# Second block: activations and products moved a few words along their buffers, by another amount in each stage

## Chip, cores and metric

One NeuronCore of one Trainium2 chip runs the whole program. The metric is device time in microseconds (us) of one execution; each kernel is timed several times and the median is given.

## The reference, cut to what matters

Two networks of two layers run one after the other on the same hidden state of 272 tokens (16 meta tokens and 256 others) by 1024 features. The second one, on the last 256 tokens, is the part that the change touches. For each of its layers:

```
h = h + 0.5 * swiglu(rmsnorm(h, g1), w_gate, w_up, w_down)      # ffn1, 1024 -> 2816 -> 1024
p = rmsnorm(h, g2) @ w_in                                       # 1024 -> 2048
h = h + mixer(p) @ w_out                                        # pooling, Fourier and attention heads
h = h + 0.5 * swiglu(rmsnorm(h, g3), w_gate2, w_up2, w_down2)   # ffn2
```

The first network (the "first block" below) has the same shape of work with 272 tokens, layer norms and another mixer.

## The kernel before

Activations lie transposed: 128 features in the partitions, tokens along the free axis, in 8 chunks for the 1024 features (`KD`) and 22 for the 2816 of the hidden layer (`NF`). A weight block of 128 by 128 is the stationary operand, an activation chunk of 128 by 256 tokens the moving one.

Every large product is made in float32r from parts. A value is split into `hi` (the value rounded to float32r) and `lo` (what is left of it), and each product of a chunk is three matmuls into the same accumulator (`three`, L620 to L624): w_lo with x_hi (L622), w_hi with x_lo (L623), w_hi with x_hi (L624). ScalarE makes the `hi` parts, VectorE the `lo` parts, of the weights as they come from HBM (double buffered in `raw`, `w_hi`, `w_lo`) and of the activations once for each stage.

A feed-forward layer has an "up" stage (22 pairs of blocks, gate and up, 8 chunks each: 22 x 2 x 8 x 3 = 1056 matmuls) that reads `x_hi` and `x_lo`, and a "down" stage (8 blocks of 22 chunks: 528 matmuls) that reads `hid_hi` and `hid_lo`, the products silu(gate) * up. The input projection has 16 blocks of 8 chunks (384 matmuls) and reads `x_hi`, `x_lo`; small float32 matmuls of the mixer are put in between its blocks by hand. The output projection (192 matmuls) reads another place of the hidden buffers. The stages of the second block in their order are up4, down4, in0, out0, up5, down5, up6, down6, in1, out1, up7, down7, where the number is `q`, the count of feed-forward layers since the start. The first two pairs of up4 are done on operands that are levelled afterwards (`plain`, 96 matmuls); the other 960 read `x_hi` and `x_lo`.

Each engine runs one list of instructions in program order with semaphores between them. TensorE waits for `x_ready` chunk by chunk at the start of a stage, for `lo_done` (the weights of a unit), `up_free` (a PSUM bank emptied) and `hid_ready`.

Where things lie is fixed by the order of allocation. `LINE` (L208) is 16 words, 64 bytes, and the buffers are spaced by gaps of one or two of them. In the second block a chunk is 256 words long and the next follows at once:

```
xt_hi, xt_lo = chunks(x_hi_all, KD, T2), chunks(x_lo_all, KD, T2)
hidt_hi, hidt_lo = chunks(hid_hi_all[:, HID_HI_T2:], NF, T2), chunks(hid_lo_all[:, HID_LO_T2:], NF, T2)
```

In each partition, in units of 64 bytes, `w_hi` begins at 610, `w_lo` at 964, the second block's `x_hi` at 1317, `x_lo` at 1465, its `hid_hi` at 2817 and its `hid_lo` at 3193. A weight block is 8 units long, a chunk of 256 tokens 16 units. So each float32r operand of the kernel, weights and activations, begins at a multiple of 64 bytes, and in the second block activations begin at an odd unit and weights at an even one. In the first block a chunk is 272 tokens (17 units) or, with columns beside it, 274, at a pitch of 17 or 18 units, and its starts are multiples of 64 bytes too. In one of its stages the three matmuls of a chunk have 258, 256 and 260 columns (L629 to L632). The constants `cst` begin 32 bytes past such a multiple; float32 matmuls read them, among them the transposes of L1182, whose moving operand is the identity at the start of `cst`.

`x_of` (L301) and `hid_of` (L307) give the pair of views that all three engines use for a stage.

Of the kernel before, what the change touches and what calls it, by code (L numbers as in the profile page):

```python
# [195 lines left out]
def build(nc, hidden0, w_up, w_down, w_in1, w_out1, w_in2, w_out2, prm1, prm2, consts, out):  # L196
    with ExitStack() as ctx:
# [103 lines left out]
        def x_of(T):  # L301
            return {T1: (x1_hi, x1_lo), T2: (xt_hi, xt_lo)}.get(T, (x_hi, x_lo))
# [4 lines left out]
        def hid_of(T):  # L307
            return (hidt_hi, hidt_lo) if T == T2 else (hid_hi, hid_lo)
# [307 lines left out]
        def _(pe):  # L616
# [83 lines left out]
            def up(q, turn0, event, T, before={}, opening=False):  # L700

                pe.wait_ge(up_free, q * NF + (CREDIT - 1))
                if opening:
                    opening_pair()
                else:
                    first_pair(turn0, event, 0, T)
                pe.wait_ge(up_free, q * NF + CREDIT)
                for u in range(2):
                    narrow_unit(turn0, 1, u, ps[:, 2 + u, 0:T], T, before=before if u == 0 else {})
                with pe.Fori(0, (UP_T - 1) // 2) as half:  # L710
                    for i in range(4):
# [3 lines left out]
                        for u in range(2):  # L715
                            narrow_unit(turn0 + half * 2 + (1 + i // 2), j, u, ps[:, 2 * j + u, 0:T], T,
# [28 lines left out]
            def crossing_up(q, turn0, event, norm, T):  # L745
# [9 lines left out]
                first_pair(turn0 + 1, event, 0, T, None, {k + 2: lambda k=k: first_square(k) for k in range(KD - 2)})  # L755
                last_squares()
                pe.wait_ge(up_free, q * NF + (CREDIT + 2))
                for u in range(2):
                    narrow_unit(turn0 + 1, 1, u, ps[:, 2 + u, 0:T], T)
                with pe.Fori(2, UP_T) as it:  # L760
                    for j in range(2):
                        pe.wait_ge(up_free, q * NF + it * 2 + (j - 1 + CREDIT))
                        for u in range(2):
                            narrow_unit(turn0 + it, j, u, ps[:, 2 * j + u, 0:T], T)
# [48 lines left out]
            def down(q, turn0, resid, T):  # L813
                ha, hb = hid_of(T)
# [278 lines left out]
            def mixer2(l, turn0, event, norm):  # L1093

                def block(i):
# [3 lines left out]
                    narrow_unit(turn0 + i // 4, (i // 2) % 2, i % 2, ps[:, i % IN_BANKS, 0:T2], T2)  # L1099
# [109 lines left out]
                first_pair(turn0, event, 0, T2)  # L1209
# [82 lines left out]
        def _(act):  # L1292
# [39 lines left out]
            def first_cast(it, j, T):  # L1332
# [3 lines left out]
                fn(hid_of(T)[0][:, f, 0:T], src, ACT.Copy).then_inc(first_casts, 1)  # L1336
# [26 lines left out]
            def high(table, gain, k, T, N):  # L1363

                fn(x_of(N)[0][:, k, 0:T], h[:, k, T1 - T:T1], ACT.Identity, scale=par(table, gain, k)).then_inc(xh_ready, 1)
# [30 lines left out]
            def down(turn0, resid, rms, norm, T, gain=None):  # L1396
                def turn(it, next_width):
                    for j in range(2):
                        split_next(turn0 + it, j, W_WIDE if j == 0 else next_width)
                        end = next_width == W_NARROW and j == 1  # L1400
                        if end and rms:

                            for k in range(KD - 1):
                                high(P2, gain, k, T, T2)
# [5 lines left out]
                        if end and rms:  # L1410
                            high(P2, gain, KD - 1, T, T2)
# [5 lines left out]
            def out_proj(turn0, resid, rms, norm, T, gain=None):  # L1417
                for p in range(OUTB // 2):
# [3 lines left out]
                    if rms and last:  # L1422

                        for k in range(KD):
                            if k >= 2 * p:
                                act.wait_ge(resid_ready, resid * KD + (k + 1 + CREDIT))
                            high(P2, gain, k, T, T2)
# [71 lines left out]
            def level_up(q, turn0, level, T):  # L1499
# [6 lines left out]
                def pair(it, j, width):  # L1506
# [11 lines left out]
                    fn(hid_of(T)[0][:, f, 0:T], prod[:, j:j + 1, 0:T], ACT.Copy).then_inc(cast_done, 1)  # L1518
# [37 lines left out]
            def crossing_up(q, turn0, T):  # L1556
# [11 lines left out]
                high(P1, "firstg", 0, T, T)  # L1568
                split_hi(turn0 + 1, 0, W_NARROW)
                for k in (1, 3, 5):  # L1570
# [3 lines left out]
                    for c in (k, k + 1):  # L1574
                        high(P1, "firstg", c, T, T)
# [1503 lines left out]
```

## Time and profile before

| | |
|---|---|
| time, median of 3 runs | 1949.19 us (1948.94 to 1949.41) |
| span of the profiled execution, first to last instruction | 1945.9 us |
| what the median has beyond that span | 3.3 us |
| TensorE busy | 1931.2 us, 99% |
| VectorE busy | 1431.5 us, 74% |
| ScalarE busy | 1019.8 us, 52% |
| mean granted TensorE clock | 0.999 |

The page gives the span of the profiled execution and no device time of its own for it. A stage is read best from the number of matmuls that start in a stretch of time: a matmul's own duration in the rows (0.28 us) overlaps its neighbours', and the distance from start to start is what it costs. The second block's stages lie about here in the span: up4 1059 to 1168 us, down4 to 1227, in0 to 1287, out0 to 1310, up5 1322 to 1442, down5 to 1501, up6 to 1621, down6 to 1681, in1 to 1735, out1 to 1757, up7 1769 to 1889, down7 to the end.

### The profile page before, as it was taken

What the parts mean: (1) busy time and instruction counts of PE and PEld (TensorE: products, weight loads), DVE (VectorE), ACT (ScalarE), POOL (GpSimd) and SP (SyncE); (2) the same over time, 40 slices, a digit from 0 to 9 for tenths busy, and PEclk for the clock granted to TensorE, in tenths of its full rate; (3) what the DMA queues carried; (4) which work ended last, traced back from release to release, by engine and by line L of the source; (5) the groups of instructions that cost most, each with busy time, mean ns of one, the idle gap of its engine ahead of it and who ended that gap; (6) DMA issues with size and microseconds to landing.
All of it is one profiled execution on the core that took longest, in us unless ns stands there. A gap on an engine that the chain in (4) does not pass through costs nothing.

```text
span 1945.9 us, 42335 instructions
## 1 busy us (share of the span) xinstructions
PE 1931.2 (99%) x16150; PEld 1892.7 (97%) x16150; DVE 1431.5 (74%) x2591; ACT 1019.8 (52%) x1527; POOL 152.7 (8%) x192
## 2 busy tenths in 40 slices
PE   9999999999999999999999999999999999999998
PEld 8999989999999999899999999999999999999998
DVE  6774787987588768879978874667765775667763
ACT  4443687554455447865547443665445444565443
POOL 0001123000100011320010100000000000100000
PEclk9999999999999999999999999999999999999999
DMA  7454433545454544345553665445555555435554
GB/s 265 172 197 170 166 109 112 192 174 193 156 192 172 196 164 145 109 152 194 201 191 140 235 233 183 151 149 185 193 214 177 195 202 208 152 131 195 194 213 154
DMA packets 46830, 346.66 MB, mean 178 GB/s; under 512 B 5344, under 2 KB 6416, under 8 KB 9232
## 3 DMA queue, kind: packets, MB, share of 16 engines
q1 hardware_dynamic: 44416, 335.63, 48.0%
q0 software_dynamic: 2320, 9.74, 1.6%
q8 instruction: 63, 1.03, 0.2%
q14 instruction: 31, 0.25, 0.0%
HBM read 344.29 MB, written 1.07 MB: 177 GB/s over the span
## 4 chain that ended last, share of the span: by engine, by line
PE 91%; DVE 4%; ACT 2%; DVEq 1%; issue 1%; DMA 0%; ACTq 0%; SPq 0%; POOL 0%
PE ps L622 22%; PE ps L623 22%; PE ps L624 22%; PE ps L639 14%; PE ps L630 2%; PE ps L631 2%; PE ps L632 2%; DVE w_lo L1996 1%; PE ps L1162 0%; DVE pj L2465 0%; DMA h<-in_hidden 0%; DVE cst L2486 0%; PE ps L1197 0%; DVE pj L2462 0%; ACT scratch L1669 0%
## 5 line engine op out<-in xcount | busy, mean ns | idle before, releaser
L1996 DVE TENSOR_TENSOR w_lo<-raw,w_hi 128x1024 fp32r<-128x1024 f32 (+1 forms) x582 | 749.3, 1313 | 151.1 <-ACT w_hi L1300 91.5
L622 PE MATMUL ps<-x_hi,w_lo 128*128 128x256 f32 (+3 forms) x2208 | 622.1, 282 | 1.5 <-DVE x_lo L2087 0.6
L624 PE MATMUL ps<-x_hi,w_hi 128*128 128x256 f32 (+3 forms) x2208 | 615.1, 279 | 0.0
L623 PE MATMUL ps<-x_lo,w_hi 128*128 128x256 f32 (+3 forms) x2208 | 614.8, 278 | 0.0
L1297 ACT ACTIVATE w_hi<-raw 128x1024 fp32r<-128x1024 f32 x454 | 466.3, 1052 | 92.5 <-PE ps L639 49.0
L622 PE MATMUL ps<-hid_hi,w_lo 128*128 128x256 f32 (+1 forms) x1536 | 431.5, 281 | 0.1
L624 PE MATMUL ps<-hid_hi,w_hi 128*128 128x256 f32 (+1 forms) x1536 | 430.2, 280 | 0.0
L623 PE MATMUL ps<-hid_lo,w_hi 128*128 128x256 f32 (+1 forms) x1536 | 429.8, 280 | 0.0
L622 PEld LDWEIGHTS ps<-x_hi,w_lo 128*128 128x128 f32 x2208 | 414.9, 188 | 6.4 <-issue 4.2
L623 PEld LDWEIGHTS ps<-x_lo,w_hi 128*128 128x128 f32 x2208 | 415.0, 188 | 0.5
L624 PEld LDWEIGHTS ps<-x_hi,w_hi 128*128 128x128 f32 x2208 | 414.6, 188 | 0.0
L622 PEld LDWEIGHTS ps<-hid_hi,w_lo 128*128 128x128 f32 x1536 | 288.7, 188 | 2.6 <-DVE hid_lo L2731 1.4
L624 PEld LDWEIGHTS ps<-hid_hi,w_hi 128*128 128x128 f32 x1536 | 288.8, 188 | 0.0
L623 PEld LDWEIGHTS ps<-hid_lo,w_hi 128*128 128x128 f32 x1536 | 288.3, 188 | 0.0
L639 PE MATMUL ps<-plain,w_hi 128*128 128x274 f32 x1280 | 211.6, 287 | 0.0
L1348 ACT ACTIVATE silu<-silu 128x256 f32<-128x256 f32 (+1 forms) x108 | 45.3, 420 | 270.6 <-DVE silu L2010 270.5
L639 PEld LDWEIGHTS ps<-plain,w_hi 128*128 128x128 f32 x1280 | 179.9, 188 | 0.0
L1300 ACT ACTIVATE w_hi<-raw 128x1408 fp32r<-128x1408 f32 x128 | 169.0, 1368 | 3.6 <-PE ps L624 2.5
L639 PE MATMUL ps<-plain,w_lo 128*128 128x274 f32 x640 | 131.7, 287 | 0.0
L639 PEld LDWEIGHTS ps<-plain,w_lo 128*128 128x128 f32 x640 | 100.1, 188 | 0.0
L2099 DVE SCALAR_TENSOR_TENSOR h<-h,ps 128x256 f32<-128x256 f32 (+2 forms) x72 | 30.0, 422 | 94.3 <-PE ps L624 94.2
L630 PE MATMUL ps<-plain,w_lo 128*128 128x258 f32 x352 | 98.2, 284 | 0.0
(351 smaller groups left out, 2315.3 us busy)
## 6 DMA issues: line engine op xcount, KB each, us to landing
raw<-in_w_up SPq DMA_DIRECT2D x176, 1024.0 KB, 4.8
raw<-in_w_down SPq DMA_DIRECT2D x64, 1408.0 KB, 6.0
raw<-in_w_in SPq DMA_DIRECT2D x36, 1024.0 KB, 4.8
raw<-in_w_out SPq DMA_DIRECT2D x16, 1024.0 KB, 4.8
cst<-row_copy POOLq DMA_DIRECT2D x2, 1088.0 KB, 8.5
raw<-in_w_up SPq DMA_DIRECT2D x4, 512.0 KB, 7.2
cst<-in_consts POOLq DMA_DIRECT2D x1, 1537.5 KB, 6.5
prm<-in_prm POOLq DMA_DIRECT2D x2, 690.0 KB, 7.2
```

The lines of the kernel that those rows point to most:

```text
L622: mm(dst, low, xa, start=first, stop=False)
L623: mm(dst, high, xb, start=False, stop=False)
L624: return mm(dst, high, xa, start=False, stop=last)
L630: mm(dst[:, 0:T2 + 2], low, xa[:, 0:T2 + 2], start=False, stop=False)
L631: step = mm(dst[:, 0:T2], high, xb[:, 0:T2], start=False, stop=False)
L632: return step if first else mm(dst, high, xa, start=False, stop=last)
L639: last = mm(dst, w[:, c, :], x[:, c, 0:T], start=w is low and c == 0, stop=w is high and x is xa and c == KD - 1)
L1297: fn(narrow_at(w_hi, place, j, u), narrow_raw(j, u), ACT.Copy).then_inc(hi_done, 1)
L1300: fn(w_hi[:, j, c], raw[:, j, c], ACT.Copy).then_inc(hi_done, 1)
L1348: fn(silu[:, j, 0:T], silu[:, j, 0:T], ACT.Silu).then_inc(silu_done, 1)
L1996: v.tensor_tensor(dst, src, high.bitcast(F32), ALU.subtract).then_inc(lo_done, 1)
L2099: v.scalar_tensor_tensor(out=dst, in0=dst, scalar=alpha, in1=ps[:, bank:bank + 1, 0:T], op0=ALU.mult, op1=ALU.add).then_inc(resid_ready, 1)
```

## The change

`x_of` and `hid_of` get the name of the stage and, for the stages in two tables, begin their views some words further on in the same buffers. Producers (ScalarE's `high` and casts, VectorE's `low` and the hid parts) and TensorE use the same views. No instruction is added or taken away, no wait is changed, and lengths and pitches stay.

| stage | hi part moved by | lo part moved by |
|---|---|---|
| up4, without its first two pairs | 32 bytes | 32 bytes |
| in0 | 16 | 16 |
| up5 | 48 | 48 |
| up6 | 96 | 96 |
| in1 | 8 | 8 |
| up7 | 32 | 0 |
| down5 | 32 | 32 |
| down6 | 16 | 16 |
| down7 | 0 | 32 |

Weights, down4, both output projections and the first block stay where they are.

```diff
+        X_WORDS = {"up4": (8, 8), "in0": (4, 4), "up5": (12, 12), "up6": (24, 24), "in1": (2, 2), "up7": (8, 0)}
+        HID_WORDS = {5: (8, 8), 6: (4, 4), 7: (0, 8)}
+
-        def x_of(T):
+        def x_of(T, stage=None):
+            if T == T2 and stage:
+                high, low = X_WORDS[stage]
+                return chunks(x_hi_all[:, high:], KD, T2), chunks(x_lo_all[:, low:], KD, T2)
             return {T1: (x1_hi, x1_lo), T2: (xt_hi, xt_lo)}.get(T, (x_hi, x_lo))
...
-        def hid_of(T):
+        def hid_of(T, q):
+            if T == T2 and q in HID_WORDS:
+                high, low = HID_WORDS[q]
+                return chunks(hid_hi_all[:, HID_HI_T2 + high:], NF, T2), chunks(hid_lo_all[:, HID_LO_T2 + low:], NF, T2)
             return (hidt_hi, hidt_lo) if T == T2 else (hid_hi, hid_lo)
...
+                xs = x_of(T, None if opening else f"up{q}")
...
-                    first_pair(turn0, event, 0, T)
+                    first_pair(turn0, event, 0, T, xs)
...
-                    narrow_unit(turn0 + i // 4, (i // 2) % 2, i % 2, ps[:, i % IN_BANKS, 0:T2], T2)
+                    narrow_unit(turn0 + i // 4, (i // 2) % 2, i % 2, ps[:, i % IN_BANKS, 0:T2], T2, x_of(T2, f"in{l}"))
...
-                fn(x_of(N)[0][:, k, 0:T], h[:, k, T1 - T:T1], ACT.Identity, scale=par(table, gain, k)).then_inc(xh_ready, 1)
+                fn(x_of(N, stage)[0][:, k, 0:T], h[:, k, T1 - T:T1], ACT.Identity, scale=par(table, gain, k)).then_inc(xh_ready, 1)
...
-                down(t0 + SEC2["ffn1"] + UP_T, r0, True, s0, T2, "mixg")
+                down(t0 + SEC2["ffn1"] + UP_T, r0, True, s0, T2, "mixg", f"in{l}")
```

The rest of the diff hands the stage's name down to `high` and `low` and to TensorE's `crossing_up`, `down` and `mixer2`.

## Rows read from the trace of the kernel before

**Rows 1.** The page: busy time of each engine; granted TensorE clock in forty slices.

```profile
PE 1931.2 (99%) x16150; PEld 1892.7 (97%) x16150; DVE 1431.5 (74%) x2591; ACT 1019.8 (52%) x1527; POOL 152.7 (8%) x192
...
PEclk9999999999999999999999999999999999999999
```

**Rows 2.** The page: shares of the chain that ended last, by engine.

```profile
PE 91%; DVE 4%; ACT 2%; DVEq 1%; issue 1%; DMA 0%; ACTq 0%; SPq 0%; POOL 0%
```

**Rows 3.** Windows of ten stretches of the second block: bounds, length, busy time (instructions) per engine, clock, DMA, GB/s.

```profile
1070.00:1160.00 90.00, 90.00 (x796) 90.00 (x796) 71.17 (x123) 41.07 (x52) 7.04 (x13) 1.00 0.67 231
1170.00:1225.00 55.00, 55.00 (x488) 55.00 (x487) 28.48 (x30) 25.33 (x30) 4.46 (x6) 1.00 0.52 188
1230.00:1285.00 55.00, 55.00 (x451) 52.17 (x450) 40.35 (x97) 32.91 (x71) 3.33 (x2) 1.00 0.41 151
1325.00:1440.00 115.00, 115.00 (x1017) 115.00 (x1016) 88.95 (x145) 51.73 (x64) 0.00 (x0) 1.00 0.58 207
1445.00:1500.00 55.00, 55.00 (x485) 54.95 (x485) 28.59 (x32) 27.04 (x35) 5.77 (x8) 1.00 0.52 184
1505.00:1620.00 115.00, 115.00 (x1017) 115.00 (x1016) 88.56 (x144) 51.17 (x63) 0.00 (x0) 1.00 0.57 203
1625.00:1680.00 55.00, 55.00 (x485) 54.95 (x484) 29.08 (x35) 27.16 (x36) 6.00 (x8) 1.00 0.50 182
1685.00:1735.00 50.00, 50.00 (x399) 46.23 (x399) 35.04 (x88) 29.46 (x68) 0.00 (x0) 1.00 0.43 154
1770.00:1885.00 115.00, 115.00 (x1017) 115.00 (x1016) 90.19 (x148) 51.96 (x63) 0.00 (x0) 1.00 0.58 204
1890.00:1938.00 48.00, 47.96 (x422) 47.55 (x420) 19.62 (x18) 19.53 (x24) 4.45 (x6) 1.00 0.45 164
```

**Rows 4.** Timeline of TensorE, first and last of 37 matmuls in a row.

```profile
1099.76 0.28 PE L622 MATMUL ps<-x_hi,w_lo 128*128 128x256 f32 x1
...
1103.84 0.28 PE L622 MATMUL ps<-x_hi,w_lo 128*128 128x256 f32 x1
```

**Rows 5.** Windows of five stretches of the first block.

```profile
40.00:120.00 80.00, 80.00 (x649) 80.00 (x648) 58.22 (x96) 32.86 (x41) 0.00 (x0) 1.00 0.51 182
160.00:200.00 40.00, 40.00 (x323) 40.00 (x322) 17.08 (x16) 13.63 (x15) 7.55 (x10) 1.00 0.45 161
360.00:440.00 80.00, 80.00 (x651) 80.00 (x650) 70.03 (x140) 42.71 (x56) 0.00 (x0) 1.00 0.51 184
560.00:620.00 60.00, 60.00 (x479) 60.00 (x478) 51.77 (x102) 31.22 (x41) 0.00 (x0) 1.00 0.51 179
880.00:940.00 60.00, 60.00 (x507) 60.00 (x506) 54.82 (x110) 32.14 (x44) 0.00 (x0) 1.00 0.53 191
```

**Rows 6.** Timeline of TensorE in the input projection, around two groups of float32 matmuls.

```profile
1269.25 0.60 PE L1182 MATMUL ps<-cst,scratch 128*128 128x128 f32 x4
1269.69 1.03 PE L1197 MATMUL ps<-scratch 128*128 128x256 f32 x4
1270.55 0.38 PE L1172 MATMUL ps<-cst,pj 128*128 128x128 f32 x2
...
1270.89 0.28 PE L623 MATMUL ps<-x_lo,w_hi 128*128 128x256 f32 x1
...
1271.61 0.28 PE L623 MATMUL ps<-x_lo,w_hi 128*128 128x256 f32 x1
...
1272.19 0.28 PE L622 MATMUL ps<-x_hi,w_lo 128*128 128x256 f32 x1
...
1273.43 0.28 PE L624 MATMUL ps<-x_hi,w_hi 128*128 128x256 f32 x1
```

**Rows 7.** VectorE groups by line, 1080 to 1160 us: busy, mean ns, idle before.

```profile
L2012 DVE SCALAR_TENSOR_TENSOR prod<-ps,rstd 128x256 f32<-128x256 f32 x15 | 6.4, 424 | 10.1 <-PE ps L624 10.1
...
L2041 DVE TENSOR_TENSOR hid_lo<-prod,hid_hi 128x256 f32 x14 | 6.0, 426 | 2.4 <-issue 2.4
L2039 DVE CAST hid_hi<-prod 128x256 f32 (+1 forms) x15 | 4.4, 294 | 2.8 <-issue 2.7
```

More of the change, by code:

```diff
@@ L1403, in turn @@
                             for k in range(KD - 1):
-                                high(P2, gain, k, T, T2)
+                                high(P2, gain, k, T, T2, stage)
                         if end:
@@ L1410, in turn @@
                         if end and rms:
-                            high(P2, gain, KD - 1, T, T2)
+                            high(P2, gain, KD - 1, T, T2, stage)
                 with act.Fori(0, DOWN_T - 1) as it:
@@ L2082, in up, with low @@
                 turn(UP_T - 1, W_WIDE)
-            def low(number, table, gain, k, T, N):
-                xa, xb = x_of(N)
+            def low(number, table, gain, k, T, N, stage=None):
+                xa, xb = x_of(N, stage)
                 dve.wait_ge(xh_ready, number * KD + (k + 1))
@@ L2219, in level_up, with down @@
                 pair(UP_T - 1, 1, None)
-            def down(turn0, alpha, T, number=None, gain=None):
+            def down(turn0, alpha, T, number=None, gain=None, stage=None):
                 def turn(it, next_width):
@@ L2228, in turn @@
                             for k in range(KD - 1):
-                                low(number, P2, gain, k, T, T2)
+                                low(number, P2, gain, k, T, T2, stage)
                         if end:
@@ L2238, in down @@
                 if gain:
-                    low(number, P2, gain, KD - 1, T, T2)
+                    low(number, P2, gain, KD - 1, T, T2, stage)
             def last_down(turn0):
@@ L2251, in last_down, with out_proj @@
                 turn(DOWN_T - 1, True)
-            def out_proj(turn0, alpha, T, banks, number=None, gain=None):
+            def out_proj(turn0, alpha, T, banks, number=None, gain=None, stage=None):
                 for p in range(OUTB // 2):
@@ L2260, in out_proj @@
                             for k in ((0, 1, 2), (3,))[u]:
-                                low(number, P2, gain, k, T, T2)
+                                low(number, P2, gain, k, T, T2, stage)
                         elif last and u == 1:
@@ L2267, in out_proj @@
                     for k in range(4, KD):
-                        low(number, P2, gain, k, T, T2)
+                        low(number, P2, gain, k, T, T2, stage)
                     lo_unit(turn0 + OUTB // 4, 1, 0, W_NARROW)
```

49 lines of the change are left out of this document (25 added, 24 removed).

## The prediction

> **What bounds the kernel.** I read the page's first two parts before anything else. TensorE is busy 99% of the span and its granted clock stands at 9 tenths or more in every slice [rows 1], so the clock is not in play, and the chain that ended last is TensorE for 91% [rows 2]. A change that touches neither the number of matmuls nor a wait can then move the time in one way: by what one matmul costs from start to start. So the views that matter are the windows, which count matmuls in a stretch, and the timeline.
>
> In the second block the count is the same wherever only float32r products run: 1017 matmuls in each of three stretches of 115 us in up5, up6 and up7, 796 in 90 us in up4, 485 in 55 us in down5 and down6 [rows 3]. The exact distance is read from the timeline: 36 matmuls from 1099.76 to 1103.84 us, 4.08 / 36 = 113.3 ns [rows 4]. At 2.4 GHz, the level that the full granted clock means, 256 columns take 106.7 ns, so 6.6 ns of each matmul are no column time. In the input projections the count is lower (451 in 55 us, 399 in 50 us) since longer float32 matmuls stand between.
>
> **What the change can touch.** Counting the matmuls whose moving operand is moved: up4 960, up5, up6 and up7 3 x 1056 = 3168, in0 and in1 2 x 384 = 768, down5, down6 and down7 3 x 528 = 1584; together 6480. One nanosecond on each is 6.5 us of the whole, and 0.2% of the time, 3.9 us, which is about what a measurement of this kernel can tell from no change, is 0.6 ns on each. So the whole prediction is: what happens to these 6.6 ns when a moving operand begins 8, 16, 32, 48 or 96 bytes further on.
>
> **The parts that cost nothing.** The same number of instructions is issued, the transfers don't change, and no wait is added, so nothing is queued anew on SP's or POOL's queue. ScalarE and VectorE write and read the moved views with instructions of unchanged shape. No row shows a store at such an offset, so I bound it: VectorE's two operations on the hidden parts take 0.43 and 0.29 us for each of the pairs, and ahead of the same pair's up product it waits 10.1 us in 15 pairs for TensorE, 0.67 us each [rows 7]. They would have to double before TensorE noticed. If that cover were gone, each tenth of their time would be 0.07 us for each of 3 x 22 pairs, 5 us. I take 0, and nothing speaks for a gain here, as VectorE is not what sets the end.
>
> **The part that may cost: the moving operand's phase.** No row of before has a float32r operand off a multiple of 64 bytes. The nearest rows give these bounds.
>
> First, that distances between the operands matter at all. The first block's stages run with the same three matmuls and other distances of 64-byte units: 649 matmuls of 272 columns in 80 us are 123.3 ns each, 10.0 above their 113.3 of columns; 323 in 40 us are 123.8, 10.5 above; 651 of 274 columns in 80 us 122.9, 8.7 above their 114.2; 479 in 60 us 125.3, 11.1 above; and 507 of 258, 256 and 260 in 60 us 118.3, 10.8 above the mean of 107.5 [rows 5]. Against 6.6 in the second block that is 2.1 to 4.5 ns more. Two streams read at once, the moving operand and the weights of the next matmul, and how they meet has a price.
>
> Second, that the price is not a property of one address alone. After float32 matmuls in in0 the float32r ones run at (1271.61 - 1270.89) / 6 = 120 ns for a while, and then at (1273.43 - 1272.19) / 11 = 113 ns, in the same block, at the same kind of addresses [rows 6]. The pair of streams starts out of step and slides into a place where it collides less. In a stage of chunks of 256 columns each matmul repeats the phase of the one before, so a place once found is kept for thousands of matmuls. A shift by a part of 64 bytes changes where the moving stream steps from one 64-byte unit to the next; if the streams can slide, they find a place again at the same price. The second block gives that price in `x` stages and in `hid` stages, which have different distances to the weights (1317 and 2817 against 964, in units). That is the reason for my value: 0 ns.
>
 Put on 6480 matmuls it is 10.4 us. It has a second use: 1.7 ns is the least that a matmul costs above its columns here, so at most 6.6 - 1.7 = 4.9 ns are to be won, 4.9 x 6480 = 32 us.
>
> Fourth, the far end: a chunk of 1024 bytes that begins inside a unit touches 17 units instead of 16. If a unit costs its 16 columns' time however little of it is used, that is 6.7 ns, 43 us in all.
>
> On the resettling after float32 groups in in0 and in1: one case costs about 6 x 6.7 = 40 ns, the kernel puts some 18 groups into each projection, 0.7 us; halved or doubled it is 1 us at most over both, inside the noise.
>
> The Trainium skill, "TensorE: Matmul & The Clock Gate", section "Back-to-back issue gap", gives a warm gap of N / 2.4 + 2.5 ns, 109.2 for 256 columns. This trace has 113.3, so here it does not hold as it stands; an estimate by it of what shifts could win at best is 4.1 x 6480 = 27 us.
>
> The same skill, "SBUF — State Buffer", section "Door 1: The DMA port swizzle", says that SBUF lines are 16 bytes long and that each step to a new line costs. By it a shift of a multiple of 16 bytes changes nothing, as a chunk still covers 64 lines, and only in1, at 8 bytes, touches a 65th. No run here shows it yet. It sides with my value, and it would set in1 apart, which has 384 of the 6480 matmuls.
>
> **The sum.** Span 1945.9 us, with 0 for the stores and 0 for the 6480 matmuls: 1945.9. The median has 3.3 us beyond the span, so 1949.2.
>
> **The rivals.**
>
> *A start inside a unit has a small price of its own.* For: four rows of L1182 read 1.6 ns more than L1197. Against: the reading is coarse and the stream there is half as fast. Time: 0.6 to 2 ns, 4 to 13 us, so 1953 to 1962. Chance 0.17.
>
> *The streams collide as in the first block.* The shifted moving operand and the weights meet in the pattern of the first block's stages and stay in it, since each matmul repeats the phase. For: five stages of the first block, each dearer. Against: there chunk lengths or pitches are other than 16 units, so phases wander; in the second block they do not. Time: 2.1 to 4.5 ns on all, 14 to 29 us, so 1963 to 1978. It decides the sign from 0.6 ns on, or from about a fifth of the matmuls at 3 ns. Chance 0.15.
>
> *A seventeenth unit is paid in full.* Time: 6.7 ns on each would be 43 us, 1992; in up7 a third of the matmuls and in down7 two thirds read an unmoved part, 704 in all, which takes off 5 us: 1988. Against: in the first block 274 columns, which touch 18 units, cost no more above their columns than 272, which touch 17 (8.7 and 11.1 against 10.0 and 10.5). Chance 0.08.
>
> *Faster: the 6.6 ns are themselves a collision that a shift inside the unit opens.* Every distance so far is a whole number of units, and half a unit might let weights and activations pass between each other. For: 1.7 ns suffices for a slow stream, and even the best float32r stretch has 6.6. Against: 6.6 is met in stages with different distances, like a floor of this stream. If all stages gained all, 1917; the amounts differ by stage, so a half of it, or half of the stages, is the likelier, 1933, and a quarter 1941. Chance 0.22.
>
> **How the numbers follow.** No change has 0.38 and is the likeliest single case, with its own range of 1945.3 to 1953.1. The slower rivals together have 0.17 + 0.15 + 0.08 = 0.40, the faster one 0.22. The range leaves out 0.08 below 1937, the greater part of a full gain, and 0.1 above 1984, the full seventeenth unit and a bit of collisions worse than the first block's: 1937 to 1984. Different stages may go different ways, and then the sum lies inside.
>
> **What the profile of the changed kernel would show.** Windows over the same ten stretches, set to the stages' new places, are the test: 1017 matmuls in 115 us means no change in that stage; 978 would be 4.3 ns more, 1056 as much less. Down4 must stay at 488 in 55 us, being unmoved. If the price hangs on the shift, up5 (48), up6 (96) and up7 (32 and 0) will differ, though they are the same work; if it hangs on crossing a 16-byte line, only in1 moves. Up7 and down7 tell by lines L622 to L624 whether it is the moved part alone that pays. Wrong would be the idea that the streams slide into an equally good place: a steady distance other than 113.3 ns in a moved stage, with TensorE still without waits. A longer wait for `x_lo` or `hid_lo` before a stage would show that the stores were dearer, which I exclude.

## The result, and the profile after

The changed kernel takes 1981.79 us (median of 4, 1979.47 to 1981.96) against 1949.3 for the kernel before (median of 4): 1.0166 times as long, 95% interval 1.0151 to 1.018. I had forecast no change. The time lies inside my range, on the side of the slower rivals.

The page has nothing to explain it but TensorE itself, 35 us more busy time at the same clock (against [rows 1]):

```profile
PE 1966.4 (99%) x16150; PEld 1927.9 (97%) x16150; DVE 1431.8 (72%) x2591; ACT 1019.6 (51%) x1527; POOL 152.8 (8%) x192
...
PEclk9999999999999999999999999999999999999999
```

The windows over the same ten stretches, set to the stages' new places, answer to [rows 3]; columns as there:

```profile
1075.00:1160.00 85.00, 85.00 (x720) 85.00 (x720) 63.72 (x107) 37.45 (x48) 6.94 (x13) 1.00 0.62 216
1180.00:1235.00 55.00, 55.00 (x486) 55.00 (x485) 29.97 (x31) 25.68 (x32) 5.19 (x7) 1.00 0.47 167
1237.00:1292.00 55.00, 55.00 (x439) 52.16 (x438) 39.95 (x97) 31.67 (x68) 3.32 (x2) 1.00 0.40 147
1330.00:1445.00 115.00, 115.00 (x974) 115.00 (x973) 87.27 (x147) 50.76 (x63) 0.00 (x0) 1.00 0.53 191
1455.00:1510.00 55.00, 55.00 (x467) 55.00 (x466) 29.12 (x31) 24.74 (x31) 5.19 (x7) 1.00 0.44 163
1520.00:1635.00 115.00, 115.00 (x969) 115.00 (x969) 86.60 (x144) 51.28 (x62) 0.00 (x0) 1.00 0.54 193
1645.00:1700.00 55.00, 55.00 (x465) 55.00 (x464) 27.83 (x30) 24.13 (x30) 5.18 (x7) 1.00 0.45 162
1705.00:1760.00 55.00, 55.00 (x428) 51.79 (x427) 38.90 (x94) 30.34 (x68) 2.30 (x2) 1.00 0.39 136
1795.00:1910.00 115.00, 115.00 (x988) 115.00 (x987) 88.79 (x149) 52.35 (x65) 0.00 (x0) 1.00 0.55 197
1922.00:1970.00 48.00, 48.00 (x403) 48.00 (x402) 18.33 (x16) 19.52 (x24) 4.45 (x6) 1.00 0.45 164
```

Down4 in the second line, which was not moved, has 486 matmuls in 55 us where before had 488, with a count that is good to one or two. Every moved stage has fewer: up4 720 in 85 us, where before has 796 in 90, up5 974 in 115 us for 1017, up6 969, up7 988, down5 and down6 467 and 465 in 55 us for 485, down7 403 in 48 us for 422. VectorE's (DVE) and ScalarE's (ACT) share of the span falls with it, and nobody waits for anything new.

Two things said of before have to be set right for this reading. A window counts the matmuls that are running in it, not only those that start in it, so two or three that were under way at its beginning are in the count: 1017 in 115 us is (115 + 0.28) / 1017 = 113.4 ns, and 974 is 118.4. And up5, down5, up6, down6 and up7 begin some 11 us earlier in the span of before than was said (up5 at 1311 us, down5 1431, up6 1491, down6 1611, up7 1757, down7 1877), so that the stretches of [rows 3] for up5 to down6 and up7 hold some 9 us of the stage behind them. In before the price there is the same within 1 ns, so the counts stand. The stretches shown below for other kernels also reach up to 13 us into the next stage; the prices in the text don't, they are taken from the records of one stage alone.

From the start times of all records of a stage (distances over 160 ns, which are a wait or another matmul in between, are left out) the mean distance from one matmul to the next is, in ns:

| stage | moved by (hi, lo), bytes | before | after | stage longer by, us |
|---|---|---|---|---|
| up4 | 32, 32 | 113.6 | 118.3 | 4.5 |
| down4 | 0, 0 | 113.3 | 113.4 | 0.0 |
| in0 | 16, 16 | 114.1 | 118.8 | 1.7 |
| up5 | 48, 48 | 113.4 | 118.3 | 5.2 |
| down5 | 32, 32 | 113.3 | 118.3 | 2.7 |
| up6 | 96, 96 | 113.4 | 118.9 | 5.9 |
| down6 | 16, 16 | 113.3 | 118.9 | 2.9 |
| in1 | 8, 8 | 114.1 | 121.3 | 2.7 |
| up7 | 32, 0 | 113.4 | 116.7 | 3.5 |
| down7 | 0, 32 | 113.3 | 120.0 | 3.5 |

The sum is 32.6 us, 5.0 ns on each of the 6480 matmuls. The spans differ by 34.2 (1980.1 and 1945.9); the other 1.6 us are in the first block, which the change does not touch, and they are a difference of two parts. The profiled execution of before waited 1.1 us longer in its first microseconds; the first line is before's, the second the changed kernel's:

```profile
PE ps L677 <- DVE x_lo L2812: 1.5, 1, 1.5
PE ps L686 <- DVE x_lo L2823: 0.4, 1, 0.4
```

Against it stand about 2.6 us more in one up stage of the first block. There the profiled executions fell on two sides of something that the program does with and without the change. The changed kernel has:

```profile
380.00:440.00 60.00, 60.00 (x478) 60.00 (x478) 50.36 (x99) 30.57 (x40) 0.00 (x0) 1.00 0.49 177
560.00:620.00 60.00, 60.00 (x479) 60.00 (x477) 51.70 (x105) 31.52 (x41) 0.00 (x0) 1.00 0.49 175
```

The first of these stretches has 489 matmuls in the kernel before. I come back to it at the end.

In down7 only the lo part was moved. The lines L622 to L624 of before are L631 to L633 in the changed kernel. From L632, w_hi with hid_lo, the next matmul starts 0.13 us later, from its neighbours 0.12:

```profile
1932.16 0.28 PE L633 MATMUL ps<-hid_hi,w_hi 128*128 128x256 f32 x1
1932.28 0.28 PE L631 MATMUL ps<-hid_hi,w_lo 128*128 128x256 f32 x1
1932.40 0.28 PE L632 MATMUL ps<-hid_lo,w_hi 128*128 128x256 f32 x1
1932.53 0.28 PE L633 MATMUL ps<-hid_hi,w_hi 128*128 128x256 f32 x1
```

Over the stage it is 124 ns after L632, 119 after L631 and 117 after L633. So the matmul that reads the moved part pays most, but the two that read an unmoved one pay too, 4 to 6 ns above before's 113.3. How the price is shared among the three lines is not fixed: with the same addresses down7 of the eighth experiment below has 121, 118 and 114. The stage's mean is what to read.

### The profile page after: what moved, and what is told of

Read it like the earlier page. It is cut to its first block, busy times and chain, and to the rows that moved or that the text cites. A ratio compares the mean times of both kernels' runs of the same rounds, so it can differ in the third digit from the quotient of the medians.

```text
span 1980.1 us, 42335 instructions
## 1 busy us (share of the span) xinstructions
PE 1966.4 (99%) x16150; PEld 1927.9 (97%) x16150; DVE 1431.8 (72%) x2591; ACT 1019.6 (51%) x1527; POOL 152.8 (8%) x192
## 4 chain that ended last, share of the span: by engine, by line
PE 91%; DVE 4%; ACT 2%; DVEq 1%; issue 1%; ACTq 0%; DMA 0%; SPq 0%; POOL 0%
PE ps L631 22%; PE ps L633 22%; PE ps L632 22%; PE ps L648 14%; PE ps L639 2%; PE ps L640 2%; PE ps L641 2%; DVE w_lo L2007 1%; PE ps L1173 0%; DVE pj L2476 0%; DVE cst L2497 0%; PE ps L1208 0%; DVE pj L2473 0%; ACT scratch L1680 0%; DVE scratch L2442 0%
## 5 line engine op out<-in xcount | busy, mean ns | idle before, releaser
L631 PE MATMUL ps<-x_hi,w_lo 128*128 128x256 f32 (+3 forms) x2208 | 630.3, 285 | 1.5 <-DVE x_lo L2098 0.6
L633 PE MATMUL ps<-x_hi,w_hi 128*128 128x256 f32 (+3 forms) x2208 | 623.3, 282 | 0.0
L632 PE MATMUL ps<-x_lo,w_hi 128*128 128x256 f32 (+3 forms) x2208 | 622.1, 282 | 0.0
L1308 ACT ACTIVATE w_hi<-raw 128x1024 fp32r<-128x1024 f32 x454 | 466.2, 1052 | 111.7 <-PE ps L648 50.3
L631 PE MATMUL ps<-hid_hi,w_lo 128*128 128x256 f32 (+1 forms) x1536 | 434.6, 283 | 0.1
L632 PE MATMUL ps<-hid_lo,w_hi 128*128 128x256 f32 (+1 forms) x1536 | 433.3, 282 | 0.0
L633 PE MATMUL ps<-hid_hi,w_hi 128*128 128x256 f32 (+1 forms) x1536 | 432.4, 282 | 0.0
L631 PEld LDWEIGHTS ps<-x_hi,w_lo 128*128 128x128 f32 x2208 | 415.6, 188 | 6.3 <-issue 4.2
L632 PEld LDWEIGHTS ps<-x_lo,w_hi 128*128 128x128 f32 x2208 | 417.2, 189 | 0.5
L633 PEld LDWEIGHTS ps<-x_hi,w_hi 128*128 128x128 f32 x2208 | 415.6, 188 | 0.0
L631 PEld LDWEIGHTS ps<-hid_hi,w_lo 128*128 128x128 f32 x1536 | 288.9, 188 | 2.5 <-DVE hid_lo L2742 1.3
L633 PEld LDWEIGHTS ps<-hid_hi,w_hi 128*128 128x128 f32 x1536 | 290.1, 189 | 0.0
L632 PEld LDWEIGHTS ps<-hid_lo,w_hi 128*128 128x128 f32 x1536 | 288.6, 188 | 0.0
L2023 DVE SCALAR_TENSOR_TENSOR prod<-ps,rstd 128x256 f32<-128x256 f32 (+1 forms) x108 | 46.1, 427 | 82.7 <-PE ps L633 82.7
L1385 ACT ACTIVATE pj<-h (+1 forms) x48 | 19.7, 417 | 157.7 <-DVE h L2110 157.7
```

The costliest lines, as they stand in the source:

```text
L631: mm(dst, low, xa, start=first, stop=False)
L632: mm(dst, high, xb, start=False, stop=False)
L633: return mm(dst, high, xa, start=False, stop=last)
L1308: fn(narrow_at(w_hi, place, j, u), narrow_raw(j, u), ACT.Copy).then_inc(hi_done, 1)
L2023: v.scalar_tensor_tensor(out=half, in0=upb[:, 0:T], scalar=0.5, in1=rstd[:, 0:T], op0=ALU.mult, op1=ALU.mult).then_inc(up_free, 1)
```

## The experiments

Four theories were open after the result. A: a start inside a 64-byte unit costs, whatever the weights do. A16: crossing a 16-byte line costs. B: the distance between the moving operand and the weights costs. S: any move off the old placement costs. Since the stages up5, up6 and up7 are the same work, and down4 to down7 too, one kernel can try another placement in each. Each kernel but the last is the changed one with the edit shown. Prices below are mean distances in ns as in the table. Experiments 1 to 6 and 9 to 11 were executed once each. How good such a price is can be seen from the stages that were left alone: up and down stages of 256 columns at the old distance have 113.3 to 113.6 in every run that has them, input projections 114.0 to 114.4.

### 1. Whole units of 64 bytes

```diff
-        X_WORDS = {"up4": (8, 8), "in0": (4, 4), "up5": (12, 12), "up6": (24, 24), "in1": (2, 2), "up7": (8, 0)}
-        HID_WORDS = {5: (8, 8), 6: (4, 4), 7: (0, 8)}
+        X_WORDS = {"up4": (0, 0), "in0": (0, 0), "up5": (16, 16), "up6": (32, 32), "in1": (0, 0), "up7": (16, 0)}
+        HID_WORDS = {4: (16, 16), 5: (32, 32), 6: (16, 0), 7: (0, 16)}
```

> Activations are moved by whole units of 64 bytes alone: up5 by one unit (hi and lo), up6 by two, up7 the hi part by one, down4 by one, down5 by two, down6 the hi part by one, down7 the lo part by one; up4, in0, in1 not at all. Theory A (a start inside a 64-byte unit is what costs): every stage stays at 113.3 ns for each matmul, and the time is 1949 us. Theory B (the distance between the moving operand and the weights is what costs, and 64 bytes matter as parts of them do): up6 and down5, moved by an even number of units, stay at 113.3; up5, up7 and down4, down6, down7, where activations and weights now begin at units of the same parity, go to 117 to 125 ns, and the time to some 1965 us.

Measured 1974.11 us. Up4 and the input projections were back at 113.5 and 114.1 to 114.2. Up5 and down4 (64 bytes) took 119.1, up6 and down5 (128 bytes) 118.9, up7 and down6 (hi part by 64) 117.8, down7 (lo part by 64) 117.8. Theory A is out: aligned starts cost as much as misaligned ones. B stands, but not as I had put it, for by it 128 bytes should have been free.

### 2. Small amounts

```diff
+        X_WORDS = {"up4": (1, 1), "in0": (8, 8), "up5": (4, 4), "up6": (8, 8), "in1": (8, 8), "up7": (14, 14)}
+        HID_WORDS = {4: (1, 1), 5: (2, 2), 6: (12, 12), 7: (14, 14)}
```

> Both parts moved by 4 bytes (up4, down4), 8 (down5), 16 (up5), 32 (up6, in0, in1), 48 (down6) and 56 (up7, down7). Theory A (any start inside a 64-byte unit costs the same, since a chunk then touches 17 units): all moved stages at 118 to 119 ns. Theory A16 (crossing 16-byte lines costs beside it): 16, 32 and 48 bytes at 118 to 119, and 4, 8 and 56 bytes dearer by 2 to 3 ns, 121, as in1 was in the changed kernel. Theory B (the phase between the two streams): the price rises and falls with the amount, so 4 bytes would be near 113.3 to 114 and 32 bytes the most. By each the two input projections, moved by 32 bytes here, come to about 118 ns between their float32 groups. Time 1978 to 1990 us.

Measured 1989.86 us. Multiples of 16 bytes: 118.9 (16), 118.3 (32 in up6, 118.4 and 118.3 in in0 and in1), 118.3 (48). Others: 121.2 and 121.5 (4 bytes), 121.6 (8), 120.2 and 120.0 (56). So the price jumps with the first 4 bytes and does not grow with the amount, and what is not a multiple of 16 bytes costs some 1 to 3 ns more. A16 had foreseen this, beside the larger price. Whether it comes from lines of 16 bytes or from the distance to the weights is not shown, as no run moved activations and weights together by such an amount. In1 of the changed kernel, moved by 8 bytes, had 121.3 and comes down to 118.3 here at 32.

### 3. The weights moved instead

```diff
+        sb("gapw", [P, LINE // 2])
         w_hi = sb("w_hi", [P, 2, 2 * W_WIDE], F32R)
...
-        sb("gap0", [P, LINE])
+        sb("gap0", [P, LINE // 2])
...
+        X_WORDS = {"up4": (0, 0), "in0": (8, 8), "up5": (8, 8), "up6": (0, 0), "in1": (0, 0), "up7": (4, 4)}
+        HID_WORDS = {4: (0, 0), 5: (8, 8), 6: (12, 12), 7: (16, 16)}
```

> Both weight buffers are moved 32 bytes further on in the whole program; activations: up5, in0 and down5 moved 32 bytes too, so that their distance to the weights is the old one; up4, up6, in1 and down4 not moved; up7 by 16 bytes, down6 by 48, down7 by 64. Theory A (the moving operand's own start costs): up4, up6, in1 and down4, down7 at 113.3 ns, up5, down5, up7, down6 at 118 to 119, whatever the weights do; the first block as before. Theory B (the distance to the weights costs): up5, down5 at 113.3 and up4, up6, down4 at 118 or more, and the first block changes too. A third possibility, each stream pays for its own misplaced start: up6 and up4 about 118, up5 and down5 more than either, 120 to 124.

Measured 1978.16 us. Windows of up5, down5 and up6 (115, 50 and 115 us):

```profile
1335.00:1450.00 115.00, 115.00 (x1017) 115.00 (x1016) 91.11 (x151) 52.64 (x65) 0.00 (x0) 1.00 0.56 203
1455.00:1505.00 50.00, 50.00 (x443) 50.00 (x442) 27.27 (x29) 22.87 (x28) 4.47 (x6) 1.00 0.49 177
1515.00:1630.00 115.00, 115.00 (x979) 115.00 (x978) 87.39 (x147) 50.69 (x63) 0.00 (x0) 1.00 0.53 191
```

Up5 and down5, whose activations and weights are both off by 32 bytes, have the old 1017 matmuls in 115 us: 113.4 and 113.3 ns. Up6, whose activations lie where they always did, has 979: 117.8, as have up4 and down4. Down6 is a distance of +16 bytes and takes 118.9, down7 +32 and takes 118.3, the same as those distances cost in the second experiment. Up7 is -16 bytes and takes 117.8. This is theory B without a remainder: the distance to the weights counts, and the moving operand's own address does not.

### 4. Fewer columns

```diff
                 xs = x_of(T, None if opening else f"up{q}")
+                T = {5: 248, 6: 248, 7: 240}.get(q, T)
...
                 ha, hb = hid_of(T, q)
+                T = {5: 248, 6: 248, 7: 240}.get(q, T)
...
+        X_WORDS = {"up4": (0, 0), "in0": (0, 0), "up5": (0, 0), "up6": (8, 8), "in1": (0, 0), "up7": (0, 0)}
+        HID_WORDS = {5: (0, 0), 6: (8, 8), 7: (8, 8)}
```

> Leaves out the last 8 or 16 tokens of the matmuls of four feed-forward layers' stages (their results are left as they were in PSUM): up5 and down5 248 columns from an unmoved start, up6 and down6 248 columns from a start moved by 32 bytes (which end on a 64-byte boundary and touch 16 units), up7 240 columns from an unmoved start, down7 240 from a start moved by 32 bytes (it touches 16 units). Above the time of the columns (103.3 ns for 248, 100.0 for 240) before has 6.6 ns. Theory A1 (a chunk pays for each unit touched, 17 in place of 16): up6 and down6 have 16 units and cost no more than up5 and down5. Theory A2 (a start inside a unit costs by itself): up6 and down6 keep 11 to 12 ns above their columns, 115, and up5 is 110. Theory A3 (an end inside a unit costs as a start does): up5 and down5 are 11 to 12 above too. Up7 is 106.7 by each if nothing but full units matters; an odd number of units could cost more by theory B.

This kernel leaves out a part of the work; its time was 1950.58 us. 248 unmoved columns took 113.3 ns, exactly what 256 take; 248 moved by 32 bytes 115.6; 240 unmoved 111.9, 240 moved 112.2. None of the three theories had foreseen that 8 columns less save nothing. So the 6.6 ns that I had counted as the moving stream's own are not a surcharge on its columns.

### 5. The period

```diff
+        X_WORDS = {"up4": (192, 192), "in0": (64, 64), "up5": (64, 64), "up6": (128, 128), "in1": (80, 80), "up7": (48, 48)}
+        HID_WORDS = {4: (64, 64), 5: (48, 48), 6: (128, 128), 7: (80, 80)}
```

> Both parts moved by 256 bytes (up5, in0, down4), 512 (up6, down6), 768 (up4), 192 (up7, down5) and 320 (in1, down7). In the runs so far the price hung on the distance between activations and weights alone, and 64 and 128 bytes cost as much as 32. Before holds 113.3 ns for all chunks, though from one chunk to the next the distance changes by 512 bytes, and `x` and `hid` stages differ by 256 in the distance of their hi parts. Theory P256 (the phase repeats after 256 bytes): 256, 512 and 768 at 113.3, 192 at 117 to 119, 320 as the 64 bytes of the second experiment's up5, 119.1. Theory P512: 512 at 113.3, and 256 and 768 at 117 to 121. Theory S (any move off the placement before costs, whatever its size): all at 118 to 119. Time: 1961 us by P256, 1972 by P512, 1980 by S.

Measured 1962.14 us. Windows of up5, up6 and up7, 110 us each:

```profile
1325.00:1435.00 110.00, 110.00 (x972) 110.00 (x971) 87.52 (x147) 51.72 (x63) 0.00 (x0) 1.00 0.56 202
1505.00:1615.00 110.00, 110.00 (x973) 110.00 (x972) 86.88 (x145) 49.85 (x63) 0.00 (x0) 1.00 0.56 200
1775.00:1885.00 110.00, 110.00 (x932) 110.00 (x931) 82.89 (x142) 48.26 (x61) 0.00 (x0) 1.00 0.53 190
```

256 bytes (up5, down4), 512 (up6, down6) and 768 (up4) are free: 113.3 to 113.6. 192 bytes costs 118.4, 320 costs 119.1, as 64 did. The price repeats after 256 bytes. Theory S is out. It is also clear now why all chunks of a stage could have one price: from chunk to chunk the distance grows by 512 bytes, two periods.

### 6. Far fewer columns

```diff
+                T = {5: 192, 6: 128, 7: 224}.get(q, T)
...
+        X_WORDS = {"up4": (0, 0), "in0": (0, 0), "up5": (0, 0), "up6": (0, 0), "in1": (0, 0), "up7": (0, 0)}
+        HID_WORDS = {5: (8, 8), 6: (8, 8), 7: (8, 8)}
```

The line with `T` stands in the same two places as in the fourth experiment.

> Leaves out the last tokens in the matmuls of six stages (their results stay as they were in PSUM): 192 columns in up5 and down5, 128 in up6 and down6, 224 in up7 and down7; up stages not moved, down stages moved by 32 bytes. In the run with 248 columns the unmoved stage stayed at 113.3 ns, as with 256, which the moving stream alone can't explain. Theory W (loading the next weights sets the pace, and the moving stream only disturbs it): 128, 192 and 224 columns all lie between 107 and 113 ns, well above their column times of 53, 80 and 93, and the moved stages stand 0 to 5 ns above the unmoved, less with fewer columns, as there is less to collide with. Theory M (each matmul costs its columns and a fixed 6 to 7 ns, and 248 was a coincidence of phase): 60, 87 and 100 ns.

This kernel too leaves out a part of the work; its time was 1938.48 us. Windows of up5 (192 columns) and up6 (128), 110 us each:

```profile
1320.00:1430.00 110.00, 110.00 (x987) 110.00 (x986) 88.70 (x150) 51.91 (x65) 0.00 (x0) 1.00 0.57 205
1500.00:1610.00 110.00, 110.00 (x988) 110.00 (x986) 88.42 (x145) 51.18 (x62) 0.00 (x0) 1.00 0.57 208
```

987 and 988 matmuls in 110 us: 111.6 ns with 192 columns and with 128, where the columns alone are 80 and 53 ns. Up7, with 224, took 111.7, and so did down5 to down7, moved by 32 bytes. The loads of weights (PEld) keep this pace themselves; these two rows of up5 are the first and the last of ten, nine distances in 1.01 us:

```profile
1319.97 0.19 PEld L631 LDWEIGHTS ps<-x_hi,w_lo 128*128 128x128 f32 x1
...
1320.98 0.19 PEld L631 LDWEIGHTS ps<-x_hi,w_lo 128*128 128x128 f32 x1
```

Is it the loads that set the pace, or a least distance between any two matmuls? The trace of before has a pair of float32 matmuls with 2 moving columns each:

```profile
1238.70 0.30 PEld L1107 LDWEIGHTS ps<-pj,cst 128*128 128x128 f32 x2
1238.81 0.28 PE L1107 MATMUL ps<-pj,cst 128*128 128x2 f32 x2
```

By their start times the two loads are 112 ns apart and the two matmuls 31. So matmuls can start closer together, and loads of this size have the distance of 112 here too. Not every load has this distance: in the float32 transposes of L877 the loads, 128 columns of 64 rows, start 58 to 65 ns apart. For float32r with 128 to 224 columns I therefore take the load as what sets the pace of 111.7 ns, and there a bad distance costs nothing. What the second block pays is this pace; the moving stream adds 1.7 ns to it at the good distance and 6 to 7 at a bad one (both parts moved, by a multiple of 16 bytes), once it fills the time between two loads. The Trainium skill, "TensorE: Matmul & The Clock Gate", section "LDWEIGHTS (loading the stationary operand)", has a load take its columns divided by 1.2, 106.7 ns for 128; the pace measured here is 5 ns above that.

### 7 and 8. The halves of the change

The seventh keeps `X_WORDS` of the change and empties `HID_WORDS`, the eighth the other way round.

> Only the `x` part of the change (up4, in0, up5, up6, in1, up7), `hid` as before. If each stage pays for its own move, as the stages of the changed kernel read: 4.5 + 1.7 + 5.2 + 5.9 + 2.7 + 3.5 = 23.5 us, so 1973 us, ratio 1.012. If a part of it is made by the neighbours (a later start that collides with something else), the two halves don't add up to the whole.

> Only the `hid` part of the change (down5, down6, down7). By the stages of the changed kernel 2.7 + 2.9 + 3.5 = 9.1 us, so 1958 us, ratio 1.005.

Against before at a median of 1946.86 (8 runs): the `x` half 1970.43, ratio 1.0117 (1.01 to 1.0134), the `hid` half 1954.99, ratio 1.004 (1.0026 to 1.0054). That is 23.6 and 8.1 us, where 23.5 and 9.1 were expected; together 31.7. In the eighth down7 took 117.8 ns, where the whole change had 120.0 with the same addresses, 1.2 us over the stage; down5 took 118.9 for 118.3. A bad distance thus has more than one steady pattern.

### 9 and 10. Another distance between the weight buffers

```diff
-        sb("gap", [P, 2 * LINE])
+        sb("gap", [P, 3 * LINE])
...
+        X_WORDS = {"up4": (48, 48), "in0": (0, 0), "up5": (0, 0), "up6": (16, 16), "in1": (16, 16), "up7": (32, 32)}
+        HID_WORDS = {4: (0, 0), 5: (16, 16), 6: (32, 32), 7: (48, 48)}
```

This is the ninth; the tenth has `4 * LINE`.

> The gap between the weight buffers is one unit of 64 bytes longer, so w_lo and all that lies behind it (the activations too) are one unit further from w_hi. The activations of the second block then run through all four unit phases: moved by 0 (up5, down4), 1 (up6, down5), 2 (up7, down6) and 3 units (up4, down7). By the runs so far the phase of 256 bytes decides. Theory P (what meets is the moving stream of one matmul and the weight load of the next, so both w_hi and w_lo have a best phase against the activations): with w_hi and w_lo no longer two units apart, a phase that suits w_hi misses w_lo or the other way round, and no stage gets back to 113.3; the best is 115 to 117, the worst 121. Theory W (only the distance to one of the two weight buffers matters): one of the four phases gives 113.3. The first block changes in part: its stages at 123 to 126 ns move by 1 to 4 ns either way.

> The same with two units more between the weight buffers, so that w_hi and w_lo lie at the same phase of 256 bytes; activations again at all four phases. Theory P: one phase of four suits both buffers, and as good as before, 113.3 ns; the others 118 to 121. Theory D (the two weight buffers must be two units apart, as before has them, because consecutive weight loads would meet each other): no phase gives 113.3. If any gives less, towards the 111.7 ns that weight loads alone took in the run with fewer columns, there is a version faster than both kernels: 1.6 ns on 8000 matmuls, 13 us.

Let a phase be the place in a period of four units of 64 bytes, and let (a, b) mean that the activations are a units past w_hi and b past w_lo in it. Before is (3, 1). Ninth, 1982.77 us: (0, 1) 117.8; (1, 2) 115.6; (2, 3) 117.8 in down6 and 118.7 in up7; (3, 0) 117.8. Tenth, 1982.58 us: (1, 1) 117.8; (2, 2) 118.7; (3, 3) 113.6 in up7 and 113.4 in down6; (0, 0) 119.9 and 120.0. Windows of up5, up6 and up7 in the tenth, 115 us each:

```profile
1340.00:1455.00 115.00, 115.00 (x978) 115.00 (x978) 88.21 (x146) 51.84 (x63) 0.00 (x0) 1.00 0.56 199
1525.00:1640.00 115.00, 115.00 (x972) 115.00 (x971) 86.82 (x145) 49.87 (x62) 0.00 (x0) 1.00 0.53 190
1800.00:1915.00 115.00, 115.00 (x1014) 115.00 (x1013) 91.09 (x151) 52.33 (x64) 0.00 (x0) 1.00 0.58 202
```

The third line, 1014, is the good one. In the ninth (3, 0) has before's distance to w_hi and (0, 1) its distance to w_lo, and neither reached 113.3, so the distance to each of the two buffers matters, not to one; and the tenth shows that the two buffers need not be two units apart. Nothing was better than before, so I have no version that beats both kernels.

### 11. More columns from a fixed phase

```diff
+                W = {5: 264, 6: 272, 7: 274}.get(q, T)
...
+                                    last = three(ps[:, 2 * j + u, 0:W], high[:, k, :], low[:, k, :], wide[0][k], wide[1][k],
+                                                 k == 0, k == KD - 1)
```

`wide` are views of W columns at a pitch of 256 words; no stage is moved.

> Activations unmoved. In the loops of up5, up6 and up7 (80 of 88 units of 24 matmuls... each) the matmuls read 264, 272 and 274 columns, the last 8 to 18 of them from the next chunk, into columns of PSUM that nothing reads; the chunks stay 1024 bytes apart, so that each matmul begins at the same phase. The first block has 272 columns at a pitch of 17 or 18 units and takes 123 to 124 ns, 274 columns 123 to 125. Theory F (a fixed start phase avoids the collisions, whatever the number of columns): column time and the same 6.6 ns, 116.7, 120.0 and 120.8. Theory E (an end that does not fall on the period of 256 bytes brings collisions): 272 at 123 or more. By F the first block could win some 3 ns on 5500 matmuls, 17 us, by another pitch; by E it could not.

The loops have 40 units of 24 matmuls, 960, in each of the three stages; the bracket in the expectation has their number wrong. Windows of up5 (264 columns) and up7 (274), 105 and 100 us:

```profile
1330.00:1435.00 105.00, 105.00 (x846) 105.00 (x845) 74.88 (x126) 43.61 (x54) 0.00 (x0) 1.00 0.51 182
1800.00:1900.00 100.00, 100.00 (x792) 100.00 (x791) 70.13 (x116) 39.89 (x50) 0.00 (x0) 1.00 0.50 178
```

The time was 1984.15 us. 264 and 272 columns both took 124.5 ns, 274 took 126.7. Theory F is out: at this fixed phase, the good one for 256 columns, the first block would be no better off than it is, with 123.7 for its 272 at wandering phases by the records (the 123.3 read from [rows 5] are a window's count). E forecast the price, but its reason, that the end must fall on the period, is not shown: with 248 columns the end does not, and they took 113.3. Other fixed phases were not tried.

### 12. Everything 32 bytes further on

```diff
+        sb("gapw", [P, LINE // 2])
         w_hi = sb("w_hi", [P, 2, 2 * W_WIDE], F32R)
```

This is the kernel before with this one line.

> The kernel before with a gap of 32 bytes ahead of w_hi, so that both weight buffers and everything allocated behind them, activations included, lie 32 bytes further on: no float32r operand begins at a multiple of 64 bytes any more, and all distances between operands are the old ones. If only the distance between the moving operand and the weights counts: 113.3 ns in every stage of the second block, the first block as before, and the time that of before within 0.2%, ratio 1.000 (0.9985 to 1.0015, with the 2.5 us between the two levels at which before itself was seen). If a start inside 64 bytes had a price of its own beside it: 1.01 or more. Of the two levels of before, 1946.7 and 1949.2, the first block's second up stage is the likely cause: 60 us of it hold 489 matmuls or 479.

Ratio 1.0003, 0.9993 to 1.0012 (10 runs against 13 of before). No float32r operand begins at a multiple of 64 bytes, and nothing is lost. First a stretch of the first block, then up5 with 13 us of down5:

```profile
380.00:440.00 60.00, 60.00 (x478) 60.00 (x478) 50.07 (x99) 30.32 (x40) 0.00 (x0) 1.00 0.47 171
1330.00:1445.00 115.00, 115.00 (x1018) 115.00 (x1017) 88.23 (x142) 52.67 (x63) 0.00 (x0) 1.00 0.56 205
```

By the records all up and down stages of the second block have 113.3 to 113.6 ns.

## Why the prediction was wrong where it was

**What held.** TensorE was the only thing to look at; the number of moved matmuls, 6480, and the idea to read it stage by stage were right (9 stages, 32.6 us). Stores cost nothing: no wait appeared. That they and their engines play no part is also seen in down5 of the changed kernel, where the matmuls with both VectorE and ScalarE idle until the next one starts are 118.2 ns apart (136 of them), and those with both at work in that time as well (145). The first bound, that distances between operands matter and that it is two streams that meet, was the mechanism. The test that I named, 978 matmuls in 115 us for 4.3 ns more, came out at 974. That the time lies within the range at all is owed to the slower rivals, which were given 0.40 between them; the value itself, 0 ns, was 32.6 us off, and the step on which it rested failed.

**The step that failed** is the second bound: "if the streams can slide, they find a place again at the same price". They do find a steady pattern, since each moved stage is constant from beginning to end, but it is a dearer one. I had two reasons. One was that `x` and `hid` stages have the same price at different distances. By the period of 256 bytes they are at the same distance, for 1317 and 2817 units both leave 1 when divided by 4, and so do 1465 and 3193. The rows had one point where I read several. The other was that after float32 groups the stream returns to 113 ns [rows 6]. It returned to the good pattern because the addresses allowed it: in in0 of the changed kernel, between the same groups, the mean is 118.8.

**The third and fourth bounds** were about the wrong thing. A start inside a unit has no price of its own (experiments 3 and 12), and a seventeenth unit has none either: up5 of experiment 3 begins inside a unit, touches 17, and takes 113.4. L1182's 1.6 ns was a coarse reading. By the start times its four matmuls are 109.0 ns apart, 2.3 above their columns, and the four of L1197 215.0 to 216.7, 1.7 to 3.4 above theirs.

**The rival that came closest** is the collision pattern of the first block. Its mechanism was right and its size short: 2.1 to 4.5 ns, against 5.0 on average and 4.7 to 5.6 where both parts moved by a multiple of 16 bytes. The 0.5 ns on 6480 matmuls are 3 us beyond its upper end of 1978. They were lost in reading: I divided a stretch by its count as if only matmuls that start in it were counted. With the 0.28 us added, the stages of [rows 5] have 80.28 / 649 = 123.7, 40.28 / 323 = 124.7, 80.28 / 651 = 123.3, 60.28 / 479 = 125.8 and 60.28 / 507 = 118.9 ns, which is 2.5 to 5.1 ns more above their columns than 6.6, and the rival's time would have been 1965 to 1982.

**The floor.** I took 6.6 ns as the moving stream's surcharge and gave 0.22 to winning it back. Experiment 6 shows that 5.0 of it is the pace of weight loads (111.7 - 106.7), which was the same with activations unmoved and moved; 1.7 ns are left, and none of the placements tried won them.

**Issue gap, ports and lines.** The issue gap of N / 2.4 + 2.5 ns did not hold for the float32r matmuls of any run. The Trainium skill, "TensorE: Matmul & The Clock Gate", section "Back-to-back issue gap", gives it for a matmul by itself and says beside it that in a stream of loads and matmuls both set the spacing; I had passed over that, and experiment 6 agrees with it. The Trainium skill, same page, section "Part 2: What happens when you issue a matmul", also says that the two read ports of TensorE are independent and that a load of weights does not take bandwidth from the running matmul. The measurement decides against it for these float32r matmuls: moving nothing but the weights by 32 bytes cost 4.5 ns (experiment 3). The 16-byte lines of the Trainium skill, "SBUF — State Buffer", section "Door 1: The DMA port swizzle", may be what shows in experiment 2 as 1 to 3 ns for starts that are not a multiple of 16 bytes away, but only beside the larger price; my reading of it as "a multiple of 16 bytes changes nothing" was wrong.

**The sum.** I wrote that the median has 3.3 us beyond the span. Executions with both numbers show 1.8 (1981.93 and 1980.1). The profiled execution of before, some 1947.7 us by that, was shorter than the three timed ones: it had the faster pattern of which the last section tells, and lost 1.1 us of it again by its wait at the start.

**What stays open.** Why some phases suit and others do not, in terms of how the memory is divided: the runs give a period of 256 bytes and a price for each distance, and no more. Why a bad distance has several steady patterns is open too.

## What to carry to other kernels

When loads of weights and a stream of moving columns take nearly the same time, their distance in memory is a parameter of the kernel: measure it as matmuls in a fixed stretch, stage by stage, and keep it when a buffer is moved. Here it repeats after 256 bytes and has to be right for each weight buffer in use; alignment to 64 bytes by itself is worth nothing. And know what a view counts: matmuls running in a stretch taken for matmuls starting in it were half a nanosecond on each of them here. And before the constancy of a number is taken as a floor, ask whether the rows differ in what matters: a stage with fewer columns would have told at once whose 6.6 ns they were.

## What the runs showed of the hardware that I had not expected

The same program with the same addresses has two levels. Of the 13 runs of the kernel before beside the last experiment 7 lie at 1946.3 to 1947.0 us, 4 at 1949.0 to 1949.5 and 2 elsewhere, and the twelfth kernel's 10 runs lie at 1946.5 to 1946.7 and 1949.0 to 1949.6. In the stretch from 380 to 440 us, inside an up stage of 1056 matmuls whose operands no kernel but the third, ninth, tenth and twelfth moved, the profile of before has 489 matmuls in 60 us. So has the eighth, profiled at the lower of its levels (1954.86 us):

```profile
380.00:440.00 60.00, 60.00 (x489) 60.00 (x488) 51.27 (x102) 30.85 (x41) 0.00 (x0) 1.00 0.49 178
```

The changed kernel and the twelfth (1949.2 us) have 478, and so nearly has the seventh (479), whose profiled execution was the longest of its four, 1973.36 us against 1970.4. By the start times it is one distance or the other, 123.3 or 126.0 ns: 123.3 in the profiles of before and of experiments 1, 2, 6 and 8, 126.0 in those of the changed kernel and of 4, 5, 7, 11 and 12. Over the stage that makes 2.6 us, the distance of the levels. The link rests on the four kernels named, whose profiled execution can be placed at a level; no kernel has a profile at each. The four times of before in the result are all at its upper level, and so are three of the four of the changed kernel, so their medians compare like with like. Before's own next stage of that kind has 479 [rows 5], with the same addresses: the streams can settle in either pattern and keep it for a whole stage. What decides between them is open.
